# Second input projection on 528 tokens: two 264-column products in place of a 512- and a 16-column one, and one reordering on GpSimd

## The chip, the cores and the metric

The kernel runs on one core of one Trainium2 chip. The metric is device time in microseconds (us) for one execution; lower is better. The core's engines run side by side, each taking its own instructions in order and meeting the others only through semaphores: TensorE (PE, with its weight loads as PEld), VectorE (DVE), ScalarE (ACT), GpSimd (POOL) and SyncE, which issues the DMAs (SP).

## What is computed

A sequence of 512 tokens of width 1024 passes through two layers of a first network and then one layer of a second. The change is in the input projection of the second network's layer. That layer sees 16 further meta tokens ahead of the 512, so keys, values, the forget gate and the pooled branch need 528 columns, while queries are only needed for the 512. Cut to what matters:

```python
n1 = rmsnorm(h, norm1_w)                       # h: 16 meta tokens + 512 tokens
proj = n1 @ w_in                               # 1024 -> q 512 | k 512 | v 512 | fg 8 | u 512
q = rmsnorm(q.reshape(B, L, 8, 64), q_norm_w)  # per head
k = rmsnorm(k.reshape(B, L, 8, 64), k_norm_w)
cum_logf = cumsum(log_sigmoid(fg + b_fgate))
a_out = forgetting_attention(q, k, v, cum_logf)
pooled = trailing_mean(u, window) - u          # windows 2, 4, 8, 16, one per group of 128
p_out = einsum(pooled, w_pool) * pool_scale
h = h + concat(a_out, p_out) @ w_out
```

The reference is float32. The kernel keeps that accuracy by splitting every operand in two: a high part rounded to the fp32r type and a low part that holds the rest. A product is then three fp32r matmuls: high x high, high x low, low x high.

The other place touched is the first network's convolution module: u = a * sigmoid(g), a depthwise convolution of 31 taps, a layer norm.

## The kernel before

Activations lie with features on the partitions and tokens in the free dimension, so a tile is 128 output features by 512 tokens, one PSUM bank (PS has eight banks, 0 to 7). Weights come in blocks of 128 x 1024 floats, that is one output tile of all eight k-steps. A ring of four slots carries them: SP loads `raw`, ACT rounds it to `wh` (the helper `hi(n)`), POOL subtracts to get `wl` (`lo(n)`), PE uses both. Block n may be rounded only once PE is done with block n - 4.

**The stretch changed most.** The second projection, phases `w_in_2` and `w_in_2b`, has on PE: tiles 0 to 3 (queries, entered together with the operand's making), tile 4 (forget gate), 5 to 8 (the pooled branch's u), 9 and 10 (keys of heads 0 to 3), then the small `pool` block (four products with `w_pool`), two further key tiles (heads 4 to 7), and the value stage, where tokens are the stationary side and a 16-row product serves the meta tokens. Each of the nine tiles from 4 on (seven in `w_in_2`, two in `w_in_2b`) is made by `tile(..., meta_out=...)`: 24 products of 512 columns into one bank of four taken in turn (`T % 4`), and, inserted into k-steps 4 to 7, 24 products of 16 columns for the meta tokens into bank 5 or 7 (`meta_bank`). So k-steps 4 to 7 hold three wide and six narrow products. Before the first narrow one PE waits until the evacuation of tile T - 2 is over (`bank_free`).

DVE scales the 512 columns by the row norm (`r2`) on the way out of PSUM; the meta columns are normalised already, so they are copied by an instruction of their own. The head norms of q and k need PE twice more, hooked into the tiles: `head_stat(e)` (sums of squares by eight to ten tiny products) and `head_spread(e)` (four transposes that broadcast 1/rms, in `hexp`, back over the partitions). Between them ACT takes the root (`head_root`) and DVE inverts and expands it (`head_factor`: RECIPROCAL, then COPY to `hexp`; for keys two more for the meta tokens). After the spread DVE multiplies (`head_norm`), ACT rounds (`head_round`) and DVE makes the low part (`head_low`). DVE also does `log_forget`, `prefix_sums`, `pool_tile(i)` (i + 1 additions over 528 columns and a final operation, giving `pooled`), and `pool_out(i)`. ACT's `pool_operand(t)` and a POOL subtraction split `pooled` for PE. All these are written out by hand in one fixed order for each engine; no scheduler moves them.

**The other stretch.** In the convolution module (`pw1`), PE goes through the tiles a0, g0, a1, g1, a2, c0, g2, a3, c1, g3, a4, ... (weights of a and g, and the taps that PE takes, c). DVE forms `tmp`, ACT the sigmoid, DVE `U`, ACT its high part `UH` and next the roundings `hi`, POOL its low part `UL` (`low_u`), then POOL adds up the taps that ACT prepared (`add_taps`) and those of DVE (`add_vector_taps`), with `lo` of coming weight blocks placed between by `lo_to(n)`, which lowers all blocks below n that are not lowered yet. DVE itself works off 18 taps of each tile.

## Time and profile before

| | us |
|---|---|
| median of 3 runs | 1800.65 (1798.9 to 1801.8) |
| the profiled execution's own time | 1802.55 |
| its span in the trace | 1800.8 |
| PE busy | 1769.1 (98%) |
| POOL / DVE / ACT busy | 887.2 / 789.7 / 663.7 |

The page gives busy time by engine over the whole span; the stretches of interest are short (nine tiles of some 1800 us), so they are read from the timeline. A start time in the timeline is exact to 10 ns; the durations of PE's matmuls overlap each other, so the cost of one is the distance from its start to the next start. "idle before" names who released the engine. Granted clock 1.00 is TensorE at 2.4 GHz, 0.50 is 1.2 GHz.

### The profile page before, as it was taken

To read this page: it belongs to the slowest core of one execution; us is meant where nothing else is said; L and a number is where in the kernel's file an instruction comes from. 1 tells how busy PE (TensorE), PEld (TensorE's weight loads), DVE (VectorE), ACT (ScalarE), POOL (GpSimd) and SP (SyncE) were. 2 spreads that over 40 slices of the span, in tenths; PEclk is the share of its full clock that TensorE was granted. 3 is DMA by queue.
4 is the path that set the end of the run, shared out by engine and by line. 5 is a ranking of instruction groups with operands and counts; after the bars stand their busy time and mean duration, and the time that the engine had idled before them with its cause. 6 is when DMAs were issued, how large, how long until landed. Compare 5 with 4: busy or idle time off the path is not lost.

```text
span 1800.8 us, 23006 instructions
## 1 busy us (share of the span) xinstructions
PE 1769.1 (98%) x8243; PEld 1464.7 (81%) x8243; DVE 789.7 (44%) x1230; ACT 663.7 (37%) x1039; POOL 887.2 (49%) x476
## 2 busy tenths in 40 slices
PE   8999999999999989999999999999999999999999
PEld 6887887888888878787888888888779888888887
DVE  6458554201322489755420232247548154444200
ACT  6338543322221456445322222154248432222221
POOL 5457545444444479755444444453235644444442
PEclk9999999999999999999999999999899999999999
DMA  4531123333333122232333233321210233323331
GB/s 172 138 101 58 37 69 105 97 102 94 93 101 98 59 70 97 81 95 70 104 97 102 94 94 103 96 72 35 84 48 1 94 94 94 104 93 93 106 105 70
DMA packets 46073, 158.45 MB, mean 88 GB/s; under 512 B 5744, under 2 KB 6000, under 8 KB 46000
## 3 DMA queue, kind: packets, MB, share of 16 engines
q1 hardware_dynamic: 46000, 157.45, 28.0%
q8 instruction: 49, 0.80, 0.2%
q14 instruction: 24, 0.20, 0.0%
HBM read 153.10 MB, written 2.10 MB: 86 GB/s over the span
## 4 chain that ended last, share of the span: by engine, by line
PE 91%; DVE 4%; ACT 2%; issue 1%; POOL 1%; DMA 0%; SPq 0%; DVEq 0%; POOLq 0%; ACTq 0%
PE PS L1814 27%; PE PS L1816 27%; PE PS L1815 27%; DVE PS L1196 1%; PE PS L1909 1%; PE PS L1904 1%; PE PS L1905 1%; PE PS L2065 1%; PE PS L1824 1%; PE PS L1946 0%; PE PS L1947 0%; PE PS L1856 0%; PE PS L2088 0%; DVE PS L1188 0%; PE PS L2234 0%
## 5 line engine op out<-in xcount | busy, mean ns | idle before, releaser
L526 POOL TENSOR_TENSOR wl<-raw,wh 128x1024 fp32r<-128x1024 f32 x220 | 533.1, 2424 | 630.1 <-ACT wh L719 198.3
L1815 PE MATMUL PS<-XL,wh 128*128 128x512 f32 x1288 | 503.9, 391 | 0.0
L1814 PE MATMUL PS<-XH,wh 128*128 128x512 f32 x960 | 382.2, 398 | 9.4 <-POOL wl L595 5.3
L1816 PE MATMUL PS<-XH,wl 128*128 128x512 f32 x960 | 376.6, 392 | 0.0
L1815 PEld LDWEIGHTS PS<-XL,wh 128*128 128x128 f32 x1288 | 243.4, 189 | 48.3
L1814 PE MATMUL PS<-HH,wh 128*128 128x512 f32 x688 | 267.6, 389 | 0.0
L1815 PE MATMUL PS<-HL,wh 128*128 128x512 f32 x688 | 267.6, 389 | 0.0
L1816 PE MATMUL PS<-HH,wl 128*128 128x512 f32 x688 | 267.6, 389 | 0.0
L1814 PEld LDWEIGHTS PS<-XH,wh 128*128 128x128 f32 x960 | 181.8, 189 | 47.4 <-POOL wl L595 6.2
L705 ACT ACTIVATE wh<-raw 128x1024 fp32r<-128x1024 f32 x123 | 128.6, 1056 | 244.4 <-PE PS L1816 199.4
L1816 PEld LDWEIGHTS PS<-XH,wl 128*128 128x128 f32 x960 | 181.7, 189 | 38.7
L1188 DVE TENSOR_TENSOR tmp<-PS,r 128x512 f32<-128x512 f32 x116 | 80.0, 692 | 252.3 <-PE PS L1816 239.5
L517 POOL TENSOR_TENSOR wl<-raw,wh 128x1024 fp32r<-128x1024 f32 x45 | 109.0, 2430 | 142.1 <-ACT wh L705 142.1
L719 ACT ACTIVATE wh<-raw 128x1024 fp32r<-128x1024 f32 x68 | 72.1, 1061 | 284.3 <-PE PS L1816 284.3
L1814 PEld LDWEIGHTS PS<-HH,wh 128*128 128x128 f32 x688 | 129.1, 188 | 26.9
L1815 PEld LDWEIGHTS PS<-HL,wh 128*128 128x128 f32 x688 | 129.1, 188 | 26.9
L1816 PEld LDWEIGHTS PS<-HH,wl 128*128 128x128 f32 x688 | 129.1, 188 | 26.7
L1814 PE MATMUL PS<-XF,wh 128*128 128x512 f32 x328 | 127.9, 390 | 0.1
L1816 PE MATMUL PS<-XF,wl 128*128 128x512 f32 x328 | 127.6, 389 | 0.0
L974 ACT ACTIVATE wh<-raw 128x1024 fp32r<-128x1024 f32 x56 | 59.4, 1061 | 166.3 <-PE PS L1816 166.3
L1167 ACT ACTIVATE wh<-raw 128x1024 fp32r<-128x1024 f32 x40 | 42.5, 1062 | 159.0 <-PE PS L1816 159.0
L556 POOL TENSOR_TENSOR prob<-prob,cols 128x512 f32<-128x512 f32 (+2 forms) x64 | 57.0, 894 | 40.8 <-DVE cols L1407 40.1
(351 smaller groups left out, 2517.0 us busy)
## 6 DMA issues: line engine op xcount, KB each, us to landing
raw<-weights SPq DMA_DIRECT2D x287, 512.0 KB, 3.5
X<-x_t SPq DMA_DIRECT2D x8, 256.0 KB, 6.7
out_t<-X SPq DMA_DIRECT2D x8, 256.0 KB, 4.6
KH<-rope_h SPq DMA_DIRECT2D x4, 128.0 KB, 4.7
KL<-rope_l SPq DMA_DIRECT2D x4, 128.0 KB, 5.3
QH<-XH SPq DMA_DIRECT2D x16, 32.0 KB, 2.0
QL<-XL SPq DMA_DIRECT2D x16, 32.0 KB, 2.0
pos_i<-positions SPq DMA_DIRECT2D x1, 256.0 KB, 8.9
```

What stands on the lines that cost most here:

```text
L517: pool.tensor_tensor(wl[:, n % RING], raw[:, n % RING], wh[:, n % RING].bitcast(F32), ALU.subtract).then_inc(w_lo, 1)
L526: pool.tensor_tensor(wl[:, j], raw[:, j], wh[:, j].bitcast(F32), ALU.subtract).then_inc(w_lo, 1)
L556: pool.tensor_tensor(p, p, cols[:, u % 4, 2:3].broadcast_to(p.shape), ALU.mult).then_inc(p_done, 1)
L705: sc.activation(wh[:, j], raw[:, j], ACT.Copy).then_inc(w_hi, 1)
L719: sc.activation(wh[:, j], raw[:, j], ACT.Copy).then_inc(w_hi, 1)
L974: sc.activation(wh[:, slot], raw[:, slot], ACT.Copy).then_inc(w_hi, 1)
L1167: sc.activation(wh[:, slot], raw[:, slot], ACT.Copy).then_inc(w_hi, 1)
L1188: return v.tensor_tensor(out, a, b, op)
L1196: return v.scalar_tensor_tensor(out=out, in0=a, scalar=s, in1=b, op0=op0, op1=op1)
L1814: pe.matmul(out, wa, xa, start=start, stop=False)
L1815: pe.matmul(out, wa, xb, start=False, stop=False)
L1816: return pe.matmul(out, wb, xa, start=False, stop=stop)
```

## The change

Nine tiles now treat the 528 tokens as one row. The high and low operand buffers `XH`, `XL` and the meta operands `meta_h`, `meta_l` become views of `XHR`, `XLR`, whose rows are 576 floats long (2304 bytes); the 16 meta columns stand directly before the 512, and the tokens of every row start at a multiple of 256 bytes. Likewise `r2m` holds 16 ones ahead of `r2`.

`wide_tile` makes for each k-step six products of 264 columns: each of the three operand pairs once for columns 0 to 263 and once for 264 to 527, into two adjacent banks. Three pairs of banks, (5,6), (2,3), (0,1), are taken in turn. Before its first product a wide tile waits for the evacuation of the tile that last used its pair (three tiles earlier, mostly). The head norms move to bank 7, the values' meta product to bank 6. DVE takes all 528 columns out with one instruction (`wide_in`), so the nine small ones for the meta columns go.

The hand-written orders change too: `head_spread(4)` stands at k-step 7 in place of 6, those of 5 and 6 at 7 in place of 6 with their `head_stat` at 2 in place of 3; DVE does `head_in(4)` inside `pool_tile(3)`, right after that tile's evacuation, and `head_factor(5)` ahead of `pool_out(2)`; ACT does `head_square(4)` ahead of `pool_operand(3)`; the value stage takes its first four tiles in the order 2, 3, 0, 1.

Some small buffers move into space that is free at the time (`meta`, `meta_n`, `dw_high`, `dw_low`, `meta_x`), and one `memset` of 128 x 16 is added at the start. In `pw1`, POOL lowers the blocks up to a3 (below `n + 7`) before the first tap sums of j = 0, where it was below `n + 5`.

```diff
+        XHR = sb("XHR", [P, KT, ROW], F32R)
+        XLR = sb("XLR", [P, KT, ROW], F32R)
+        XHM, XLM = XHR[:, :, ROW - L2:ROW], XLR[:, :, ROW - L2:ROW]
+        XH, meta_h = XHM[:, :, META:L2], XHM[:, :, 0:META]
...
-                lo_to(n + 5)
+                lo_to(n + 5 if j else n + 7)
...
             pool_operand(2)
             hi(n0 + 12)
+            head_square(4)
             pool_operand(3)
-            head_square(4)
             hi(n0 + 13)
...
+            def wide_in(dst, w, T, done, rows=P):
                 v.wait_ge(blocks_done, done)
-                sig(tt(dst, PS[0:rows, T % 4], r2[0:rows, :], ALU.mult), bank_free, T + 1)
+                sig(tt(in_halves(dst), wide(w, rows), in_halves(r2m[0:rows]), ALU.mult), bank_free, T + 1)
...
-            pool_tile(3)
-            head_in(4, "w_in_2", 9)
+            pool_tile(3, lambda: head_in(4, "w_in_2", 9))
             head_factor(4)
...
-                    if meta_out is not None and k >= KT // 2:
-                        if k == KT // 2:
-                            pe.wait_ge(bank_free, meta_out - 1)
-                        for i in (2 * k - KT, 2 * k - KT + 1):
-                            ins = products(PS[:, meta_bank(T), 0:META], *weight(n, i), meta_h[:, i], meta_l[:, i],
-                                           i == 0, i == KT - 1)
...
+            def wide_tile(n, w, free, hooks={}):
+                open_block(n)
+                pe.wait_ge(bank_free, free)
+                out = wide(w)
+                for k in range(KT):
+                    if k in hooks:
+                        hooks[k]()
+                    w_high, w_low = weight(n, k)
+                    for x, y, first, last in ((w_high, XHM, True, False), (w_high, XLM, False, False),
+                                              (w_low, XHM, False, True)):
+                        for b in range(2):
+                            ins = pe.matmul(out[:, b], x, y[:, k, b * WIDE:(b + 1) * WIDE], start=first and k == 0,
+                                            stop=last and k == KT - 1)
+                ins.then_inc(blocks_done, 1)
...
-                     10: {3: head(4)[0], 6: head(4)[1]}}
+                     10: {3: head(4)[0], 7: head(4)[1]}}
+            emptied = {4: T0, 5: T0 + 3, 6: T0 + 4, 7: T0 + 5, 8: T0 + 6, 9: T0 + 7, 10: T0 + 8}
             for i in range(4, 11):
-                tile(n0 + i, T0 + i, norms.get(i, {}), meta_out=T0 + i)
+                wide_tile(n0 + i, i - 4, emptied[i], norms.get(i, {}))
```

On PE, in tile 4 around its middle, before (L1814 to L1816 are the three products; 16-column ones stand between the 512-column ones):

```order
4037 L1815 MATMUL PS<-XL,wh 128x512
4038 L1816 MATMUL PS<-XH,wl 128x512
4039 L1814 MATMUL PS<-meta_h,wh 128x16
4040 L1815 MATMUL PS<-meta_l,wh 128x16
4041 L1816 MATMUL PS<-meta_h,wl 128x16
4042 L1814 MATMUL PS<-meta_h,wh 128x16
4043 L1815 MATMUL PS<-meta_l,wh 128x16
4044 L1816 MATMUL PS<-meta_h,wl 128x16
4045 L1814 MATMUL PS<-XH,wh 128x512
```

and now, with L1899 the wide products (the row of L2260 is `head_stat(0)`):

```order
4032 L2260 MATMUL PS<-headones,head_q 128x2 x4
4033 L1899 MATMUL PS<-XHR,wh 128x264 x2
4034 L1899 MATMUL PS<-XLR,wh 128x264 x2
4035 L1899 MATMUL PS<-XHR,wl 128x264 x2
4036 L1899 MATMUL PS<-XHR,wh 128x264 x2
4037 L1899 MATMUL PS<-XLR,wh 128x264 x2
4038 L1899 MATMUL PS<-XHR,wl 128x264 x2
```

Every k-step is now the same six products; the narrow ones are gone.

On ACT, between the end of tile 8 and `head_root(4)`, before (`pool_h<-pooled` is `pool_operand`, `wh<-raw` is `hi`, `hcol<-PS` is `head_root`):

```order
505 L705 ACTIVATE wh<-raw 128x1024
506 L1071 ACTIVATE pool_h<-pooled 128x512
507 L1055 ACTIVATE head_q<-head_t 128x528
508 L705 ACTIVATE wh<-raw 128x1024
509 L1062 ACTIVATE hcol<-PS 128x8
```

and now:

```order
505 L727 ACTIVATE wh<-raw 128x1024
506 L1077 ACTIVATE head_q<-head_t 128x528
507 L1093 ACTIVATE pool_h<-pooled 128x512
508 L727 ACTIVATE wh<-raw 128x1024
509 L1084 ACTIVATE hcol<-PS 128x8
```

The square of head 4 went ahead of `pool_operand(3)`; its root stays behind both that and `hi`.

On POOL at the start of `pw1`, before (`wl<-raw,wh` is `lo`):

```order
71 L624 TENSOR_TENSOR UL<-U,UH 128x542
72 L607 TENSOR_TENSOR acc_p<-acc_p,tapped 128x512 x2
73 L595 TENSOR_TENSOR wl<-raw,wh 128x1024
74 L607 TENSOR_TENSOR acc_p<-acc_p,tapped 128x512 x2
75 L635 TENSOR_TENSOR acc_p<-acc_p,taps_sum 128x512 x2
76 L624 TENSOR_TENSOR UL<-U,UH 128x542
77 L595 TENSOR_TENSOR wl<-raw,wh 128x1024
78 L607 TENSOR_TENSOR acc_p<-acc_p,tapped 128x512 x4
79 L635 TENSOR_TENSOR acc_p<-acc_p,taps_sum 128x512 x2
80 L595 TENSOR_TENSOR wl<-raw,wh 128x1024
```

and now:

```order
72 L646 TENSOR_TENSOR UL<-U,UH 128x542
73 L617 TENSOR_TENSOR wl<-raw,wh 128x1024 x2
74 L629 TENSOR_TENSOR acc_p<-acc_p,tapped 128x512 x4
75 L657 TENSOR_TENSOR acc_p<-acc_p,taps_sum 128x512 x2
76 L646 TENSOR_TENSOR UL<-U,UH 128x542
77 L629 TENSOR_TENSOR acc_p<-acc_p,tapped 128x512 x4
78 L657 TENSOR_TENSOR acc_p<-acc_p,taps_sum 128x512 x2
79 L617 TENSOR_TENSOR wl<-raw,wh 128x1024
```

The low parts of g2 and a3 (rows 73 and 77 before) now both follow the first `UL`; that of g3, the last row, stands where it stood.

## Rows read from the trace of the kernel before

**Rows 1.** The page, chain that ended last, shares of the span by engine

```profile
PE 91%; DVE 4%; ACT 2%; issue 1%; POOL 1%; DMA 0%; SPq 0%; DVEq 0%; POOLq 0%; ACTq 0%
```

**Rows 2.** Timeline of PE, tile 4: start, duration (us), engine, line, operation, operands, shapes

```profile
1214.14 0.48 PE L1814 MATMUL PS<-XH,wh 128*128 128x512 f32 x1
...
1214.68 0.39 PE L1816 MATMUL PS<-XH,wl 128*128 128x512 f32 x1
1214.91 0.17 PE L1814 MATMUL PS<-meta_h,wh 128*128 128x16 f32 x1
...
1215.50 0.47 PE L1814 MATMUL PS<-XH,wh 128*128 128x512 f32 x1
```

**Rows 3.** Timeline of PE, products of 256 and 272 columns in the two attentions

```profile
161.41 0.28 PE L2088 MATMUL PS<-PH,VV 128*128 128x256 f32 x1
...
162.25 0.28 PE L2089 MATMUL PS<-PL,VV 128*128 128x256 f32 x1
...
1351.61 0.29 PE L1815 MATMUL PS<-K2L,Q2H 128*128 128x272 f32 x1
...
1351.87 0.22 PE L2054 MATMUL PS<-mask_r,ident_r 128*128 128x128 f32 x1
```

**Rows 4.** Timeline of DVE in the second projection

```profile
1240.45 0.71 DVE L1188 TENSOR_TENSOR pool_a<-u 128x527 f32<-128x527 f32 x1
...
1267.62 1.50 DVE L1636 COPY hexp<-hcol 128x512 f32<-128x512 f32 x1
...
1284.92 0.43 DVE L1636 COPY hexp<-hcol 128x512 f32<-128x512 f32 x1
```

**Rows 5.** Timeline of ACT, from pool_operand(3) to head_root(4)

```profile
1262.74 0.63 ACT L1071 ACTIVATE pool_h<-pooled 128x512 fp32r<-128x512 f32 x1 [6.02 <-DVE pooled L1196]
...
1265.34 1.04 ACT L705 ACTIVATE wh<-raw 128x1024 fp32r<-128x1024 f32 x1
1267.07 0.18 ACT L1062 ACTIVATE hcol<-PS 128x8 f32<-128x8 f32 x1 [0.69 <-PE PS L2234]
```

**Rows 6.** Timeline of POOL, the same stretch

```profile
1263.45 1.29 POOL L669 TENSOR_TENSOR pool_l<-pooled,pool_h 128x512 fp32r<-128x512 f32 x1 [4.24 <-ACT pool_h L1071]
1266.46 2.38 POOL L517 TENSOR_TENSOR wl<-raw,wh 128x1024 fp32r<-128x1024 f32 x1 [1.71 <-ACT wh L705]
```

**Rows 7.** Chain that ended last, in order of time: head_stat(4) on PE

```profile
1266.05 0.98 PE PS L2234 x8
```

**Rows 8.** Timeline of PE, its idle times in the second projection

```profile
1209.11 0.47 PE L1814 MATMUL PS<-XH,wh 128*128 128x512 f32 x1 [0.81 <-DVE head_t L1188]
...
1283.92 0.28 PE L1814 MATMUL PS<-meta_h,wh 128*128 128x16 f32 x1 [2.57 <-DVE sqb L1192]
...
1308.35 0.50 PE L1814 MATMUL PS<-wh,XH 128*128 128x512 f32 x1 [0.99 <-DVE head_t L1188]
```

**Rows 9.** Stretches: length, busy by engine (instructions), PE's granted clock, DMA share, GB/s

```profile
1284.90:1301.80 16.90, 16.90 (x57) 14.10 (x56) 6.09 (x17) 3.07 (x6) 2.36 (x1) 0.50 0.29 96
1308.70:1312.00 3.30, 3.30 (x9) 2.55 (x8) 2.10 (x5) 1.22 (x2) 2.00 (x1) 0.51 0.00 0
```

**Rows 10.** Timeline of PE in pw1: start of a3 and of g3

```profile
656.38 0.50 PE L1814 MATMUL PS<-XH,wh 128*128 128x512 f32 x1 [3.55 <-POOL wl L595]
...
671.07 0.50 PE L1814 MATMUL PS<-XH,wh 128*128 128x512 f32 x1 [1.76 <-POOL wl L595]
```

**Rows 11.** Timeline of ACT and, below it, of POOL in pw1

```profile
637.58 2.00 ACT L705 ACTIVATE wh<-raw 128x1024 fp32r<-128x1024 f32 x2
...
653.97 2.36 POOL L595 TENSOR_TENSOR wl<-raw,wh 128x1024 fp32r<-128x1024 f32 x1
```

**Rows 12.** Chain that ended last in pw1, in order of time, up to g3

```profile
666.11 0.76 DVE U L1196
...
667.46 1.05 ACT wh L705
668.65 2.38 POOL wl L595
```

More of the change, by code:

```diff
@@ L193, in build @@
         lat = at("lat", A, 0, [P, 5, S])
+        meta_n = at("meta_n", A, 29 * KB, [P, KT, META])
+        meta = at("meta", A, 30 * KB, [P, KT, META])
         gate_c = at("gate_c", A, 10 * KB, [P, 4, S])
@@ L226, in build @@
         ln_sq = at("ln_sq", A, 58 * KB, [P, KT, S])
+        dw_high = at("dw_high", A, 84 * KB, [P, KT, PE_TAPS], F32R)
+        dw_low = at("dw_low", nc.lookup_mloc(hexp).addr, KB, [P, KT, PE_TAPS])
         tap_low = at("tap_low", A, 76 * KB, [P, 3, SLOTS, P], F32R)
@@ L414, in head_parts, with bank_pair, wide, in_halves @@
             return H[:, h], L[:, h], headones[:, odd * HD:odd * HD + 1]
-        def meta_bank(T):
-            return (RB, META_BANK)[T % 2]
+        WIDE = L2 // 2
+        PAIRS = ((RB, HB), (2, 3), (0, 1))
+        PAIR_OF = (0, 1, 2, 0, 1, 2, 0, 1, 0)
+        HEAD_NORM, V_META = META_BANK, HB
+        assert TILE0["w_in_2"] % 4 == 1
+        def bank_pair(w):
+            return PS[:, PAIRS[w][0]:PAIRS[w][1] + 1]
+        def wide(w, rows=P):
+            return bank_pair(PAIR_OF[w])[0:rows, :, 0:WIDE]
+        def in_halves(ap):
+            return ap.rearrange("p (b n) -> p b n", b=2)
+        def pool_bank(i):
+            return bank_pair(1 + i // 2)[:, i % 2]
         def result_bank(layer, h):
@@ L502, in _ @@
             pool.memset(hexp[:, 0], 0.0).then_inc(consts, 1)
-            pool.wait_ge(consts, 4)
+            pool.memset(r2m[:, 0:META], 1.0).then_inc(consts, 1)
+            pool.wait_ge(consts, 5)
             pool.affine_select(out=ident[:], in_=ident[:], compare_op=ALU.not_equal, fill=1.0, base=0,
@@ L510, in _ @@
                 rows = slice(half * HD, (half + 1) * HD)
-                pool.wait_ge(consts, 6 + half)
+                pool.wait_ge(consts, 7 + half)
                 pool.memset(headones[rows, rows], 1.0).then_inc(consts, 1)
@@ L1078, in head_round @@
                     H, _, own = head_parts(e, odd)
-                    sc.activation(H[:, tokens], PS[:, HB], ACT.Copy, scale=own).then_inc(head_hi, 1)
+                    sc.activation(H[:, tokens], PS[:, HEAD_NORM], ACT.Copy, scale=own).then_inc(head_hi, 1)
             head_square(0)
@@ L1622, in head_in @@
                 t = head_t[:, e % 4]
-                if e < 4:
-                    out = t[:, 0:S]
-                else:
-                    v.wait_ge(blocks_done, done)
-                    step(v.tensor_copy(t[:, 0:META], PS[:, meta_bank(T), 0:META]))
-                    out = t[:, META:L2]
+                if e >= 4:
+                    wide_in(t, e + 1, T, done)
+                    return
                 v.wait_ge(blocks_done, done)
-                sig(tt(out, PS[:, T % 4], r2[:], ALU.mult), bank_free, T + 1)
+                sig(tt(t[:, 0:S], PS[:, T % 4], r2[:], ALU.mult), bank_free, T + 1)
             def head_factor(e):
@@ L1687, in prefix_sums, with pool_tile @@
                 sig(tt(decay[:, 3], logf[:, 0], f(decay[:, 2]), ALU.subtract), cum_done, 1)
-            def pool_tile(i):
+            def pool_tile(i, between=None):
                 T, done = T0 + 5 + i, n0 + 6 + i
-                v.wait_ge(blocks_done, done)
-                step(v.tensor_copy(u2[:, 0:META], PS[:, meta_bank(T), 0:META]))
-                scaled(u2[:, META:L2], T, done)
+                wide_in(u2[:], 1 + i, T, done)
+                if between:
+                    between()
                 src, w = u2, 1
@@ L1857, in spread, with tile @@
                 ins.then_inc(rb_done, 1)
-            def tile(n, T, hooks={}, meta_out=None, high=XH, bank=None, order=range(KT), begun=False, ring=4):
+            def tile(n, T, hooks={}, high=XH, bank=None, order=range(KT), begun=False, ring=4):
                 if not begun:
@@ L2259, in _ @@
             for i in range(4):
-                open_tile(T1 + i)
+                pe.wait_ge(bank_free, T0 + 9 + i // 2)
                 pe.wait_ge(pool_hi, i + 1)
                 pe.wait_ge(pool_lo, i + 1)
-                ins = products(PS[:, (T1 + i) % 4], *weight(n1, i), pool_h[:, i], pool_l[:, i], True, True)
+                ins = products(pool_bank(i), *weight(n1, i), pool_h[:, i], pool_l[:, i], True, True)
                 ins.then_inc(blocks_done if i == 3 else pool_mixed, 1)
@@ L2278, in _ @@
                         head_stat(7)
-                    for t in range(4):
+                    for t in (2, 3, 0, 1):
                         q = slice(t * P, (t + 1) * P)
                         products(PS[:, (T0 + 2 + t) % 4], XH[:, k, q], XL[:, k, q], *w, k == 0, k == KT - 1)
-                    ins = products(PS[0:META, META_BANK], meta_h[:, k], meta_l[:, k], *w, k == 0, False)
+                    if i == kk == 0:
+                        pe.wait_ge(bank_free, T0 + 2)
+                    ins = products(PS[0:META, V_META], meta_h[:, k], meta_l[:, k], *w, k == 0, False)
                 ins.then_inc(blocks_done, 1)
```

46 lines of the change are left out of this document (19 added, 27 removed).

## The prediction, made before the changed kernel ran

> **What bounds the kernel now.** I read the page's chain first: 91% of what ended last is PE [rows 1], so a microsecond taken from PE's stream counts unless another engine is just behind. The second look was PE's timeline in the nine tiles, from start to start, because PE's durations overlap. In a k-step that carries meta columns, the three 512-column products take 0.77 us, the last two starts 0.23 apart, and the six 16-column ones take from 1214.91 to 1215.50, 0.59 us [rows 2]. So a product 32 times narrower still costs half of a wide one, and the first wide one behind them costs 0.09 more. Such a step is 1.36 us, one without meta columns 3 x 0.228 = 0.68. Third, the places where PE stands still: 0.8 us ahead of tile 4, 2.57 inside the first tile of `w_in_2b`, 1.0 ahead of the value stage at 1308.35 [rows 8]. Fourth, the stretches: after the 2.57 us PE runs 16.9 us at clock 0.50 and has 3.3 us more at 0.51 at the start of the value stage [rows 9].
>
> **Part 1, the products.** Before, a tile is 4 x 1.36 + 4 x 0.68 = 8.18 us plus hooks. After, it is 48 products of 264 columns. The trace has none, but it has both neighbours: 256 columns start 0.84 / 7 = 0.120 us apart, 272 columns 0.26 / 2 = 0.130 [rows 3]. All of these load 128 x 128 weights each time, as the new ones do. I take 0.1225, near the 256-column rows, since that run is of one uniform kind; bounds 0.118 and 0.130. A tile is then 48 x 0.1225 = 5.88. Gain 2.30 a tile, **20.7 us** for nine (bounds 17.5 and 22.6). The rows of 2304 bytes and the halves that start off the 256-byte grid I price at nothing; the 256-column rows are aligned, so the upper bound of 0.130 covers some cost.
>
> A rule that speaks against it: by the Trainium skill, "TensorE: Matmul & The Clock Gate", section LDWEIGHTS, a weight load takes its columns divided by 1.2 GHz, an estimate of 107 ns for 128. Twice as many loads per wide column would set a floor of 48 x 0.107 = 5.1 us a tile. The narrow products show that floor (0.11 us apart), and 5.88 lies above it, so by the page the loads hide and the sum stands.
>
> **Part 2, the stalls that go.** Tile 4 no longer waits for DVE's first evacuation, only for the row norm: 0.8. The 2.57 us [rows 8] were a narrow product waiting in the first tile of `w_in_2b` for `pool_out(3)`, behind `head_low(4)` on DVE, held up by POOL. The new tile waits for `pool_out(1)` at its start, which DVE does right after the pool block's products; that fits. The 1.0 us before the value stage came from waiting for `head_in(7)`; the stage now starts on banks freed by `head_in(6)`. Together **4.4 us**. With these stalls goes the half clock: 16.9 us at half rate did the work of some 9.0, so 7.9, and 3.3 us the work of 1.75, so 1.6: **9.5 us**.
>
> **Part 3, the stalls that come.** DVE, ACT and POOL lose only nine copies of 0.2 us while PE loses a quarter of its time, so their hand-written chains come up against PE. I laid them out from the durations in the rows. Up to tile 9 all hooks are met within 0.2 us each (0.4 in all). The tight one is `head_spread(4)` in tile 10. Count from the end of tile 9:
> - DVE: `head_in(4)` 0.7, then the five additions and final operation of `pool_tile(3)` that are queued behind it, 5 x 0.72 [rows 4]: 4.3.
> - ACT: `pool_operand(3)` 0.65, `hi` 1.04, `head_root(4)` 0.3 with its meta part [rows 5]: at 6.3. The square moved ahead in ACT's order, but the root did not, so it still waits for `pool_operand(3)`.
> - DVE: RECIPROCAL, then the COPY to `hexp`. POOL has meanwhile begun: `pool_l` 1.29 from 5.0, then `lo` 2.38 [rows 6] until 8.7. The COPY takes 1.50 us where POOL runs and 0.43 where it doesn't, and the 1.50 end with POOL's instruction [rows 4, 6]. So it ends at about 9.1, with the two for the meta tokens at 9.6.
> - PE: three k-steps, `head_stat(4)` 1.0 [rows 7], four k-steps: 2.2 + 1.0 + 2.9 = 6.1.
>
> So PE waits **3.5 us** (2 to 4.5). By the Trainium skill, "SBUF — State Buffer", section on the two separate sides, the port pair that VectorE and GpSimd share is locked for a whole instruction; the copy's rows agree. Without that lock the wait would be 2.0 and the sum 1.5 better. One more wait I find is `head_stat(6)`, which needs `head_in(6)`, `head_round(5)` and ACT's square: 0.8. The clock should fall once behind the 3.5 us, as it did behind 2.57 and 3.55 [rows 8 to 10]. The shortest low stretch in the rows is 3.3 us, costing 1.6; it can be longer, as the 16.9 us were, but those began with narrow products, which are gone. I take 1.6 and half of another, **2.4 us** (0 to 8). Sum of the costs: 0.4 + 3.5 + 0.8 + 2.4 = 7.1.
>
> **Part 4, small things.** The value stage does the same products; its meta product waits for `head_in(7)`, which is over by then. Moved buffers and the 16-column memset lie at the start or beside PE: 0 (within 0.3). SP's waits are on `w_lo` and `heads_done`, which only come earlier in the new order, and the four-slot ring still gives a load three tiles' time, 17 us.
>
> **Part 5, POOL in pw1.** PE stood 3.55 us ahead of a3, waiting for `lo`, which POOL began at 653.97 though ACT had rounded both blocks by 639.6 [rows 10, 11]. Now a3 starts at 652.7. But the chain says that this stall was free: what released g3 at 671.07 runs through DVE's `U` (666.11), ACT's `hi`, POOL's `lo` [rows 12], and ahead of that DVE works off its taps without a gap, untouched by PE. The change moves none of it. So PE does a3, waits some 0.9 for c1's rounded weights, does c1, and then stands until the same 671.07, about 6.5 us in place of 1.76. Gain 0. From g3 on PE sets the pace, so a clock that has fallen in those 6.5 us costs in full: some 2.7 us at half rate, **1.3 us lost** (0 to 1.6). Before, the low clock after the 3.55 us lay inside the wait and cost nothing.
>
> **Sum.** 20.7 + 4.4 + 9.5 - 7.1 - 1.3 = 26.2. From the profiled execution's 1802.55 that gives 1776.3. The profiled execution is 1.9 above the median of the runs shown (1800.65), so I say **1774.5**.
>
> **Rivals.**
> - *The clock stays low* (15%). After the 3.5 us the granted clock stays at 0.50 through both key tiles and into the value stage, as it did for 16.9 us before. For: it did so with the same hooks. Against: no narrow products now. It takes back 6 to 8: 1781.
> - *DVE's chain is met* (15%). If DVE gets ahead (its additions fall between POOL's instructions), the 3.5 us shrink and the clock doesn't fall: 4 to 5 better, 1770.
> - *The wide products are slower than their neighbours* (10%): 0.135 to 0.15, by halves that start off the grid. Against: the convolution's products read at every odd offset, and PE's timeline shows their starts hardly further apart. Each 0.01 is 4.3 us, less what the stalls give back: 1781 to 1785.
> - *The other side: the load isn't hidden* (3%). If a second load of the same weights can't slip under a stream of 110 ns, the products are 0.19 apart: a tile is 9.1, 0.9 more than before, 8 for nine, less what goes with the stalls and plus part 5: some 1806. It decides from 8.18 / 48 = 0.170 on. Against: the 272-column rows.
> - *It does nothing* (2%), if DVE paced the stretch: 1800. Against: DVE idles ahead of most of its waits there.
>
> **How the numbers follow.** My forecast has 55%: 1771 to 1779. The range must take in the low clock, the slower products and the met chain: **1769 to 1784**. A measurement of this kernel tells about 0.2%, 3.6 us, from no change. Chances: faster 0.95, within 0.2% 0.02, slower 0.03.
>
> **What would show it.** Right: starts of the 264-column products 0.12 to 0.125 apart; the value stage's first product near 1282 instead of 1308.35; an idle time of 2 to 4.5 us on PE ahead of `head_spread(4)`, released by DVE; g3 still at 671, with 5 to 7 us of idle time ahead of it, and the stretch behind it at clock 0.5. Wrong: g3 earlier than 671 (then part 5 is a gain), products over 0.13 apart, no wait at the spread, or a clock of 1.00 in the phase before and a low one after.

## The result, and the profile after

| | before | after |
|---|---|---|
| median | 1801.2 us (1798.9 to 1801.9, 4 runs) | 1780.1 us (1779.1 to 1780.7, 4 runs) |
| span of the profiled execution | 1800.8 | 1778.9 |

The ratio is 0.9883, 95% interval 0.9864 to 0.9902: the change takes 21 us off. The prediction said 1774.5 (1769 to 1784), faster. The side and the range hold; the middle was 5.6 us too low, and the result lies 1.1 us outside the 1771 to 1779 that I had given my own theory. The sections below say which steps that comes from. Two executions that stood far off the others of their kernel, one of `e3_root_first` (6346.9 us) and one of `e6_four_parts` (2067.4 us, at a mean granted clock of 0.81), are left out of the medians below.

**The products.** PE's timeline in tile 4 of the kernel after (start, duration in us, engine, line, operation, operands, shapes; x2 is both halves of a row):

```profile
1210.22 0.48 PE L1899 MATMUL PS<-XHR,wh 128*128 128x264 f32 x2
1210.55 0.41 PE L1899 MATMUL PS<-XLR,wh 128*128 128x264 f32 x2
...
1211.99 0.40 PE L1899 MATMUL PS<-XLR,wh 128*128 128x264 f32 x2
1212.23 0.40 PE L1899 MATMUL PS<-XHR,wl 128*128 128x264 f32 x2
```

From 1210.55 to 1212.23 seven pairs start in 1.68 us, 0.240 a pair, 0.120 a product. A k-step is 0.72 us, where one that carried meta columns was 1.36 [rows 2] and one without 0.68.

**The waits.** All idle times of PE over 0.4 us between there and the attention (in brackets the idle time and who released it):

```profile
1235.58 1.02 PE L2260 MATMUL PS<-headones,head_q 128*128 128x2 f32 x8 [0.54 <-DVE PS L1218]
...
1261.73 0.23 PE L2269 MATMUL PS<-ident,meta_x 16*128 16x16 f32 x1 [3.85 <-DVE meta_x L1660]
1274.55 0.23 PE L2269 MATMUL PS<-ident,meta_x 16*128 16x16 f32 x1 [0.67 <-DVE meta_x L1660]
...
1278.88 0.20 PE L2258 MATMUL PS<-headones,head_q 128*16 128x2 f32 x2 [1.34 <-ACT head_q L1077]
```

These are `head_stat(3)`, `head_spread(4)`, `head_spread(5)` and `head_stat(6)`. The three of [rows 8] are gone; the value stage's first product starts at 1286.67 with no wait, 21.68 us sooner than at 1308.35. What stands behind the 3.85 us is seen on DVE, ACT and POOL, one after the other:

```profile
1255.95 0.69 DVE L1218 SCALAR_TENSOR_TENSOR pooled<-pool_a,u 128x512 f32<-128x512 f32 x1
1258.46 0.20 DVE L1654 RECIPROCAL hcol<-hcol 128x8 f32<-128x8 f32 x1 [1.82 <-ACT hcol L1088]
1258.70 2.54 DVE L1655 COPY hexp<-hcol 128x512 f32<-128x512 f32 x1
...
1256.68 0.63 ACT L1093 ACTIVATE pool_h<-pooled 128x512 fp32r<-128x512 f32 x1 [3.57 <-DVE pooled L1218]
1257.21 1.04 ACT L727 ACTIVATE wh<-raw 128x1024 fp32r<-128x1024 f32 x1
1258.16 0.16 ACT L1084 ACTIVATE hcol<-PS 128x8 f32<-128x8 f32 x1
...
1258.61 2.35 POOL L539 TENSOR_TENSOR wl<-raw,wh 128x1024 fp32r<-128x1024 f32 x1
```

ACT takes the root only after `pool_operand(3)` and `hi`; the COPY to `hexp` starts 0.09 us behind POOL's subtraction and ends 0.28 us after it, 2.54 us for what took 0.43 in another place [rows 4].

**The clock.** Stretches of the kernel after (length, PE busy, instructions, granted clock, DMA share, GB/s): behind the 3.85 us, behind the 1.34, behind `g3` in pw1, and the whole of the nine tiles.

```profile
1262.80:1266.20 3.40, 3.40 (x11) 0.50 0.32 130
1280.00:1283.30 3.30, 3.30 (x16) 0.50 0.11 19
670.60:675.60 5.00, 4.96 (x12) 0.50 0.72 222
1210.20:1286.60 76.40, 69.98 (x537) 0.96 0.28 91
```

Before, the nine tiles took 99.2 us (1209.11 to 1308.35), with 16.9 of them at half clock [rows 9]; now 76.4, with 6.7 at half clock. The value stage runs at full clock from its first product, and its first product lies 29.4 us ahead of the first score product, against 31.1.

**pw1.** PE there, after the change:

```profile
658.81 0.47 PE L1830 MATMUL PS<-UH,wh 128*128 128x512 f32 x1 [0.92 <-ACT wh L727]
...
670.64 0.79 PE L1830 MATMUL PS<-XHR,wh 128*128 128x512 f32 x1 [5.97 <-POOL wl L617]
671.23 0.63 PE L1831 MATMUL PS<-XLR,wh 128*128 128x512 f32 x1
671.66 0.63 PE L1832 MATMUL PS<-XHR,wl 128*128 128x512 f32 x1
```

`g3` starts at 670.64 where it started at 671.07 [rows 10]. This execution was 0.4 us ahead of the other already at the start of pw1 (DVE's `U` at 665.70, before 666.11 [rows 12]), so `g3` gained nothing. The idle time ahead of it has grown from 1.76 to 5.97 us, and the products behind it are 0.43 us apart, at clock 0.50, for 5 us.

### The profile page after: what moved, and what is told of

It is laid out like the page before. It is cut to its first block, busy times and chain, and to the rows that moved or that the text cites. A ratio compares the mean times of both kernels' runs of the same rounds, so it can differ in the third digit from the quotient of the medians.

```text
span 1778.9 us, 22989 instructions
## 1 busy us (share of the span) xinstructions
PE 1742.8 (98%) x8243; PEld 1448.7 (81%) x8243; DVE 793.2 (45%) x1221; ACT 662.8 (37%) x1039; POOL 886.8 (50%) x477
## 4 chain that ended last, share of the span: by engine, by line
PE 88%; DVE 6%; ACT 3%; issue 2%; POOL 1%; DMA 1%; SPq 0%; DVEq 0%; POOLq 0%; ACTq 0%
PE PS L1830 26%; PE PS L1832 25%; PE PS L1831 25%; PE PS L1899 2%; DVE PS L1218 1%; PE PS L1935 1%; PE PS L1930 1%; PE PS L1931 1%; PE PS L2091 1%; DMA raw<-weights 1%; DVE PS L1210 1%; PE PS L1840 0%; DVE XLR L1218 0%; ACT wh L727 0%; PE PS L2114 0%
## 5 line engine op out<-in xcount | busy, mean ns | idle before, releaser
L1831 PE MATMUL PS<-XLR,wh 128*128 128x512 f32 x1216 | 474.4, 390 | 0.0
L1830 PE MATMUL PS<-XHR,wh 128*128 128x512 f32 x888 | 349.0, 393 | 9.3 <-POOL wl L617 6.0
L1832 PE MATMUL PS<-XHR,wl 128*128 128x512 f32 x888 | 346.8, 391 | 0.0
L1831 PEld LDWEIGHTS PS<-XLR,wh 128*128 128x128 f32 x1216 | 229.2, 188 | 47.3
L1830 PEld LDWEIGHTS PS<-XHR,wh 128*128 128x128 f32 x888 | 167.6, 189 | 45.1 <-POOL wl L617 6.4
L1832 PEld LDWEIGHTS PS<-XHR,wl 128*128 128x128 f32 x888 | 167.4, 189 | 35.1
L1210 DVE TENSOR_TENSOR tmp<-PS,r2m 128x512 f32<-128x512 f32 x116 | 80.0, 691 | 254.7 <-PE PS L1832 241.9
```

What stands on the lines that cost most here:

```text
L1210: return v.tensor_tensor(out, a, b, op)
L1830: pe.matmul(out, wa, xa, start=start, stop=False)
L1831: pe.matmul(out, wa, xb, start=False, stop=False)
L1832: return pe.matmul(out, wb, xa, start=False, stop=stop)
```

## Experiments

For small differences a number needs care here: two traces of one kernel can lie 3 us apart (see the repetition, `c1_changed_again`). I therefore give the medians, and beside them lengths of stretches within a trace: "tiles" is from the first wide product to the first product of the value stage, 76.45 us in the kernel after.

### The reordering in pw1, taken out and done alone

`e1_pw1_undone` is the changed kernel with

```diff
-                lo_to(n + 5 if j else n + 7)
+                lo_to(n + 5)
```

> The changed kernel with its reordering on GpSimd in pw1 undone alone: POOL lowers the blocks below n + 5 before the first tap sums, as in the kernel before. My theory (part 5, now with 2.3 us from the changed kernel's trace): g3 starts near 670.7 either way, since DVE's taps, ACT and POOL lead up to it; with a3 late again (3.5 us of idle, 1.8 ahead of g3) the fall of the clock lies inside the wait, and PE comes out of pw1 some 2 us sooner: about 2 us faster than the changed kernel (1778). Rival: the earlier a3 is worth its 3.5 us, and undoing it makes the kernel slower by 3 to 4 us (1784). Rival: it makes no difference, since what follows in pw1 takes up the 2 us.

Measured 1778.8 us (1778.3 to 1780.4), 1.3 below the changed kernel's 1780.1. Its PE at the same place:

```profile
655.88 0.51 PE L1830 MATMUL PS<-XHR,wh 128*128 128x512 f32 x1 [3.52 <-POOL wl L617]
...
670.56 0.50 PE L1830 MATMUL PS<-XHR,wh 128*128 128x512 f32 x1 [1.74 <-POOL wl L617]
```

and the 5.5 us behind `g3` run at clock 1.00:

```profile
670.50:676.00 5.50, 5.44 (x24) 1.00 0.69 207
```

`g3` starts at the same time whether `a3` waited 3.5 us or not. The second projection starts at 1207.77 in this trace, 1210.22 in that of the kernel after.

`e2_pw1_alone` is the kernel before with the opposite edit.

> The kernel before with the reordering on GpSimd in pw1 alone. My theory: about 2 us slower than the kernel before (1803), g3 at its old start with some 6 us of idle ahead of it and the clock at 0.50 for some 5 us behind it. Rival: faster by 3 to 4 us (1797.5).

Measured 1804.7 us against 1800.0 for the kernel before on the same chip; ratio 1.0034 (1.0016 to 1.0053), so slower. The 4.7 us between the medians is not its price: 4 of its 12 executions took 1811 to 1815 us, where 2 of 23 of the kernel before took 1809 to 1810, and I don't know why. In its trace the idle time ahead of `g3` is 6.00 us, and the start of tile 4 moves from 1209.11 to 1211.07, 1.96 later.

`e9_together_but_pw1` and `e5_again` are a pair on one chip: the improved kernel described below, with and without the change's order in pw1.

> The version with all four edits (1769.6), but with the change's order on GpSimd in pw1. It prices the pw1 reordering beside its counterpart on the same chip. My theory: 2.0 to 2.5 us slower than the version with all four, by the half clock behind g3, 1772. Rival: no difference; the 2.5 us between single traces would then be chance.

Measured 1771.6 (1769.9 to 1773.4) against 1769.0 (1768.6 to 1773.1) for `e5_again`. The intervals of the two ratios overlap widely, so this pair's medians alone would settle nothing. The three differences of medians, 1.3, 4.7 and 2.7 us, have one sign, but not one size. What settles the size is a length inside each trace, from the start of `g3` to the first product of tile 4 (us):

| pair | order of before in pw1 | the change's order | difference |
|---|---|---|---|
| kernel before, `e2_pw1_alone` | 538.04 | 540.39 | 2.35 |
| `e1_pw1_undone`, changed kernel | 537.21 | 539.58 | 2.37 |
| `e5_again`, `e9_together_but_pw1` | 537.28 | 539.65 | 2.37 |

In all six traces `g3` itself starts between 670.0 and 671.1. So the reordering in pw1 costs 2.4 us, the half of the 5 us at clock 0.50. The rival, a gain, has nothing for it.

### The 3.85 us ahead of head_spread(4)

`e3_root_first`, the changed kernel with one step moved on ACT:

```diff
             head_square(4)
+            head_root(4)
             pool_operand(3)
             hi(n0 + 13)
-            head_root(4)
             head_round(4)
```

> The changed kernel with one step moved on ACT: head_root(4) ahead of pool_operand(3). My theory of the 3.85 us that PE stands ahead of head_spread(4): ACT's root waits behind pool_operand(3), which waits for DVE's pool_tile(3); so DVE's COPY to hexp falls into POOL's lo and takes 2.5 us in place of 0.43. With the root first, DVE's RECIPROCAL starts at once after pool_tile(3), its COPY is over before POOL begins, and the spread's wait goes from 3.85 to at most 0.3; the clock no longer falls behind it (1.6 us more). About 4 to 5.5 us faster than the changed kernel (1775). Rival: DVE's additions are the limit, and the wait stays above 2 us. Rival: the wait goes but turns up again at head_spread(5) or head_stat(6) (now 0.67 and 1.34), gain under 2 us.

Measured 1774.6 us (1773.2 to 1775.2; 1775.1 with the execution that is left out). DVE and POOL at the place:

```profile
1259.91 0.43 DVE L1655 COPY hexp<-hcol 128x512 f32<-128x512 f32 x1
1260.37 0.15 DVE L1659 RECIPROCAL hcol<-hcol 16x2 f32<-16x2 f32 x1
1260.56 1.17 DVE L1660 COPY meta_x<-hcol 16x128 f32<-16x128 f32 x1
...
1260.38 1.27 POOL L691 TENSOR_TENSOR pool_l<-pooled,pool_h 128x512 fp32r<-128x512 f32 x1 [4.24 <-ACT pool_h L1093]
```

and PE's two remaining waits, and its clock over the nine tiles:

```profile
1261.79 0.23 PE L2269 MATMUL PS<-ident,meta_x 16*128 16x16 f32 x1 [0.90 <-DVE meta_x L1660]
...
1276.37 0.20 PE L2258 MATMUL PS<-headones,head_q 128*16 128x2 f32 x2 [0.93 <-ACT head_q L1077]
...
1213.20:1282.60 69.40, 67.02 (x537) 1.00 0.32 99
```

The big COPY takes 0.43 us, and the wait falls from 3.85 to 0.90. I had expected at most 0.3: the small copy to `meta_x`, 16 x 128, now falls into POOL's `pool_l` and takes 1.17 us in place of 0.21. The clock doesn't fall at all in this stretch, and the tiles take 69.4 us, 7.0 less: 2.95 from the spread, 0.67 and 0.41 from the two later waits, and 3.3 from 6.7 us that are no longer at half clock, 7.3 in sum. So ACT's order, with the collision that it sets up between DVE and POOL, was the cause, not DVE's additions as such.

`e8_evacuate_late` undoes the change's new order on DVE instead:

```diff
-            pool_tile(3, lambda: head_in(4, "w_in_2", 9))
+            pool_tile(3)
+            head_in(4, "w_in_2", 9)
```

> The changed kernel with one part of its reordering undone on DVE: head_in(4) again behind pool_tile(3), not inside it. It asks what that part is worth. My theory, laid out from the changed kernel's trace: head_t comes 4.2 us later, so PE waits some 4 us already ahead of head_stat(4) in tile 10, and less or nothing at head_spread(4), since root, RECIPROCAL and copies run in PE's four k-steps after it, partly in POOL's lo: 4 to 6 us in all in place of 3.85, time 0 to 3 us above the changed kernel. Rival: it is worth nothing, since DVE's additions end at the same time. Rival: the order before was better: 2 us or more faster.

Measured 1781.5 us (1777.8 to 1784.2). The wait moves to `head_stat(4)`, as laid out:

```profile
1262.65 0.21 PE L2259 MATMUL PS<-headones,head_q 128*16 128x2 f32 x2 [4.33 <-ACT head_q L1077]
```

and there is none left at the spread. The tiles take 76.9 us against 76.45: the waits over 0.4 us sum to 5.8 us in place of 6.4, but the clock is low for some 9.6 us in place of 6.7. As it stands, the early `head_in(4)` of the change shows no gain that one trace could tell. It should be the step that makes the fix above possible, since the root can't be taken before `head_stat(4)`; the root first without the early `head_in(4)` was not run.

### The operand's layout

`e4_rows_528`, the changed kernel with rows of 528 floats, so that the tokens of a row start at 64, 128, 192 or 0 bytes past a multiple of 256:

```diff
-ROW = 4 * META + S
+ROW = L2
```

> The changed kernel with rows of 528 floats in place of 576, so that the tokens of a row no longer start at multiples of 256 bytes, in every phase that reads the operand. My prediction priced the alignment at nothing: products of 264 columns stay 0.120 us apart, those of 512 columns 0.228, time within 2 us of the changed kernel. Rival: products off the grid are slower; already 0.002 us on each of the several thousand products that read this operand would cost some 10 us.

Measured 1800.7 us, ratio to the kernel before 0.9995 (0.9982 to 1.0008): the whole gain is gone. My expectation failed, the rival's held in kind: this layout is slower. Groups of PE's instructions in the stretch 900:1180 (line, operands, shapes, count, busy us, mean ns), first of the kernel after, then of this one:

```profile
L1831 PE MATMUL PS<-HL,wh 128*128 128x512 f32 x255 | 99.2, 389 | 0.0
...
L1831 PE MATMUL PS<-XLR,wh 128*128 128x512 f32 x157 | 61.1, 389 | 0.0
```

```profile
L1831 PE MATMUL PS<-HL,wh 128*128 128x512 f32 x235 | 91.4, 389 | 0.0
...
L1831 PE MATMUL PS<-XLR,wh 128*128 128x512 f32 x174 | 68.8, 396 | 0.0
```

Products that read `HL`, whose layout is the same in both, are unchanged; those that read the operand last longer. By their starts they go from 0.2267 us apart (27 in 6.12 us from 889.68 on) to 0.2315 (26 in 6.02 from 889.82 on). The profile counts 888 k-steps of three such products, 328 in which one of three reads the operand (there too all starts are 0.232 apart), and some 500 more: about 4,150 products by 0.005 us, an estimate of 21 us. They are spread over the whole kernel and no single wait shows them. The 264-column products go from 0.120 to 0.123 (nine pairs in 2.21 us from 1228.06 on), though nearly all of them start off the grid of 256 bytes in both layouts.

What the run shows is the price of the layout, not yet the rule behind it. In k-steps 3 and 7 the rows of this layout start at multiples of 256 bytes, as all rows of the changed kernel do, and these k-steps are no faster: from 889.13 to 923.18 the trace has 49 k-steps in a row, and every one takes 0.69 or 0.70 us, none 0.68. Either products off the grid slow their neighbours too, as the k-steps with one such product in three suggest, or it isn't the start of a row that decides. No run here separates the two.

### What sets the distance of the products

`e7_load_apart` turns the two inner loops round, so that no two products in a row have the same weights:

```diff
-                    for x, y, first, last in (...):
-                        for b in range(2):
+                    for b in range(2):
+                        for x, y, first, last in (...):
```

> The changed kernel with the loops inside a k-step turned round: first the three operand pairs on columns 0 to 263, then the three on 264 to 527, so that no two products in a row have the same weights. My theory: each product loads its weights anyway and the load hides, so the starts stay 0.120 us apart and the time within 2 us of 1780. Rival: two products in a row on the same weights are what makes 0.120 possible, and they go apart to 0.13 or more, 4 us or more slower.

Measured 1780.2 us. The starts are 0.123 us apart (seven from 1212.81 to 1213.67), not 0.120, and the tiles take 77.0 us. That is 0.5 us of 76; the pairing is worth 0.003 us a product and isn't what makes the products fast.

`e6_four_parts` cuts each product in two of 132 columns:

```diff
                         for b in range(2):
-                            ins = pe.matmul(out[:, b], x, y[:, k, b * WIDE:(b + 1) * WIDE], ...)
+                            for c in (0, WIDE // 2):
+                                ins = pe.matmul(out[:, b, c:c + WIDE // 2], x,
+                                                y[:, k, b * WIDE + c:b * WIDE + c + WIDE // 2], ...)
```

> The changed kernel with each 264-column product of the nine tiles cut in two of 132 columns: 96 products a tile. It asks for the floor that a weight load sets. My theory: half as many columns don't halve the distance, since the 16-column products, which load as many weights, start about 0.113 apart; so 0.11 to 0.12 apart here too, a tile of 10.6 to 11.5 us in place of 5.8, and 43 to 51 us more for nine, 1823 to 1831. Rival: the distance follows the columns (0.06), the time stays near 1780, and then the narrow products before were slow for another reason than the load.

Measured 1895.6 us (1895.4 to 1905.4), ratio 1.055 (1.051 to 1.059), far above my 1823 to 1831. The distance is as I said; the clock isn't. PE's timeline early in tile 4 and a little later, four products a row:

```profile
1213.40 0.61 PE L1900 MATMUL PS<-XHR,wh 128*128 128x132 f32 x4
1213.85 0.61 PE L1900 MATMUL PS<-XLR,wh 128*128 128x132 f32 x4
...
1218.79 1.06 PE L1900 MATMUL PS<-XHR,wh 128*128 128x132 f32 x4
1219.65 1.06 PE L1900 MATMUL PS<-XLR,wh 128*128 128x132 f32 x4
```

At first a product takes 0.45 / 4 = 0.112 us, like the 16-column ones before, though it has eight times their columns. By the Trainium skill, "TensorE: Matmul & The Clock Gate", section LDWEIGHTS, loading 128 columns takes an estimated 107 ns; the 0.112 agree. That it is the load and not a fixed price of any product, the two kinds of product of `head_stat` show, both with two columns (kernel after):

```profile
1253.70 0.20 PE L2258 MATMUL PS<-headones,head_q 128*16 128x2 f32 x2
1253.84 1.05 PE L2260 MATMUL PS<-headones,head_q 128*128 128x2 f32 x8
1254.75 0.49 PE L1899 MATMUL PS<-XHR,wh 128*128 128x264 f32 x2
```

With 16 columns of weights to load two products take 0.14 us, 0.07 each; with 128 columns eight take 0.91, 0.114 each. Some 5.5 us after the first product of tile 4 (1212.04), with no idle time ahead of it, the clock falls, and each product then takes 0.213 (12 in 2.56 us from 1218.79 on); at this clock the 107 ns of the Trainium skill don't hold. It stays there:

```profile
1216.00:1220.00 4.00, 4.00 (x29) 0.72 0.71 198
1221.00:1366.00 145.00, 145.00 (x677) 0.50 0.08 23
1366.00:1376.00 10.00, 10.00 (x76) 0.90 0.29 96
```

PE is busy for all of the 145 us of the second line. The clock comes back behind the first 512-column products (the `pool` block from 1363.31 on) and falls again 17 us into the next narrow ones, with PE busy throughout. So here the clock fell twice inside an unbroken stream of narrow products with a weight load each, with no stall ahead of it.

`e10_few_narrow` asks the same of the kernel before, by leaving out 21 of the 24 narrow products of each tile:

```diff
-                        for i in (2 * k - KT, 2 * k - KT + 1):
-                            ins = products(PS[:, meta_bank(T), 0:META], *weight(n, i), meta_h[:, i], meta_l[:, i],
-                                           i == 0, i == KT - 1)
+                        if k == KT // 2:
+                            products(PS[:, meta_bank(T), 0:META], *weight(n, 0), meta_h[:, 0], meta_l[:, 0],
+                                     True, True)
```

> The kernel before with 21 of the 24 products of 16 columns left out in each of the nine tiles (the first k-step's three stay, so keys, values and the rest of the meta tokens come out wrong); waits, hooks and 512-column products are as before. It asks whether the narrow products kept the clock low for 16.9 us behind the stall of 2.57 us. Work taken out: 21 x 0.113 a tile and some 0.09 for each of three returns to 512 columns less, 2.5 to 2.6 a tile, 23 us for nine; the stall of 2.57 us grows by what POOL and DVE don't give back, 2 to 5 us. My theory: with hardly a narrow product left, the clock at 0.50 behind the stall lasts 3 to 5 us in place of 16.9, some 6 us more gained: 1773 to 1777. Rival: the low stretch lasts as long, and its cause is something else (the short pieces of the hooks, the weights just loaded): 1779 to 1783.

Measured 1785.1 us (1783.4 to 1786.6), later than either theory. PE's waits and the stretches behind them:

```profile
1257.65 0.20 PE L2232 MATMUL PS<-headones,head_q 128*16 128x2 f32 x2 [4.42 <-ACT head_q L1055]
...
1275.16 0.28 PE L1814 MATMUL PS<-meta_h,wh 128*128 128x16 f32 x1 [2.71 <-DVE sqb L1192]
```

```profile
1275.10:1278.60 3.50, 3.44 (x12) 0.56 0.50 162
1278.60:1289.10 10.50, 9.41 (x48) 0.98 0.29 100
```

Behind the same stall, 2.71 us here and 2.57 before, ahead of the same instruction, the half clock now lasts 3.4 us in place of 16.9. That was my theory. The 16.9 are no chance of one execution: in the trace of `e2_pw1_alone`, which has all narrow products, the clock is at 0.50 for 16.8 us behind the same stall. The 3.4 rest on one trace. What I had not seen is the new wait of 4.42 us at `head_stat(4)`: the old orders of DVE and ACT can't feed a PE whose tiles are that much shorter, and the wait brings a fall of the clock of its own. The nine tiles take 79.8 us, against 76.45 in the kernel after, though the products of one tile take about as long (an estimate of 24 x 0.2267 + 3 x 0.113 + 0.09 = 5.9 us against 48 x 0.120 = 5.8). So the shorter tiles and the new orders belong together.

### The repetition

> The changed kernel itself once more, so that the small differences of the other runs are taken against it on the same chip: 1780.1, as before. It also asks whether the fall of the clock near 1368 in the attention (some 1.5 us), which the first trace of the changed kernel had, comes again: if it belongs to the kernel's timing, it should; if it comes and goes from run to run, the 1.5 us are no cost of the change.

Measured 1783.3 us (1779.5 to 1783.9, six runs), 3 above the first four, so not 1780.1 again. The stretch in question, of this run and then of the first trace of the kernel after:

```profile
149.80:155.80 6.00, 5.82 (x17) 0.50 0.34 62
```

```profile
147.50:155.80 8.30, 7.85 (x41) 1.00 0.30 68
```

In the first attention the clock falls for 6 us in one execution and not in another of the same program, at the same stall of 1.33 us; it costs 3 us, which is the whole difference between these two traces (tile 4 starts at 1213.28, before at 1210.22). The stall is in all 14 traces, and the clock fell behind it in this one and in that of `e3_root_first`, in no other. The fall near 1370, in the last attention (1.5 us), came again here and in `e1_pw1_undone` and `e10_few_narrow`, but in no other trace. It stands behind a stall of 1.16 us ahead of the product of `PMH` and `VMV`, which waits for `P2L`, and this stall is in all 14 traces. In that of the kernel before it is this row, and no fall follows:

```profile
1391.71 0.39 PE L2093 MATMUL PS<-PMH,VMV 128*128 128x256 f32 x1 [1.16 <-DVE P2L L1188]
```

So the fall comes and goes from one trace to the next at an unchanged stall. Both traces of the changed kernel have it; whether it belongs to that kernel stays open.

### All edits together

`e5_all_together` is the changed kernel with the order of before in pw1, `head_root(4)` first, and:

```diff
-            def pool_tile(i, between=None):
+            def pool_tile(i, between=None, ahead=None):
...
                 assert w == WINDOWS[i]
+                if ahead:
+                    ahead()
                 sig(stt(pooled[:, i], ...), pooled_done, i + 1)
...
-            pool_tile(3, lambda: head_in(4, "w_in_2", 9))
-            head_factor(4)
+            pool_tile(3, lambda: head_in(4, "w_in_2", 9), lambda: head_factor(4))
...
-                     ... 7: {4: head(3)[0]}, ...
+                     ... 7: {5: head(3)[0]}, ...
-                wide_tile(n0 + i, 7 + i, (T1 + 2, T1)[i], {2: head(5 + i)[0], 7: head(5 + i)[1]})
+                wide_tile(n0 + i, 7 + i, (T1 + 2, T1)[i], {2 + i: head(5 + i)[0], 7: head(5 + i)[1]})
```

> The changed kernel with four edits: the reordering in pw1 undone, head_root(4) ahead of pool_operand(3), head_factor(4) ahead of the last operation of pool_tile(3) on DVE, and head_stat(3) and head_stat(6) one k-step later. My theory, in which PE sets the pace: against the root-first kernel (1775.1), 2.0 to 2.5 for pw1 and up to 0.9 + 0.5 + 0.7 for the waits that were left: about 1771. The wait at head_spread(4) goes (0.9 in the root-first kernel, since the small copy to meta_x still fell into POOL's instruction). Rival: the gains don't add, since a stall in pw1 or at the spread is paid again by the clock or by a later wait: 1774 to 1776.

Measured 1769.6 us, ratio to before 0.9828 (0.9806 to 0.9850); the changed kernel on the same chip has 0.9895 (0.9875 to 0.9915). Repeated:

> The version with all four edits once more, as the counterpart of the one before it: 1769.6 again, about 10 us below the changed kernel. It also asks whether the wait of 1.2 us that its first trace showed in the last attention, ahead of a product that reads P2L, belongs to it.

Measured 1769.0, ratio 0.9821 (0.9797 to 0.9845). In the repetition the nine tiles take 67.8 us at full clock, with one wait left over 0.4 us, ahead of `head_spread(3)`; the one that the question was about is in the last attention:

```profile
1238.90 0.66 PE L2272 MATMUL PS<-ident,hexp 128*128 128x128 f32 x4 [0.53 <-DVE hexp L1655]
...
1357.75 0.39 PE L2120 MATMUL PS<-PMH,VMV 128*128 128x256 f32 x1 [1.15 <-DVE P2L L1210]
```

It doesn't belong to this version: the kernel before has the same wait, 1.16 us (above), and so has every other trace. Moving `head_stat(3)` only moved its wait, 0.54 to 0.53, to the spread behind it. It is the fastest version of this study, some 11 us below the changed kernel's first runs and 31 below the kernel before.

## Why the prediction was right, and where it was off

- **Part 1, the products: right, a little low.** 0.120 us apart, predicted 0.1225 (0.118 to 0.130). Nine tiles of 48 give 73.6 - 51.8 = 21.8 us, predicted 20.7. The floor set by the load hides under 264 columns, as said; `e6_four_parts` shows it coming out below that. The layout "priced at nothing" was right for the change as made, but not because the layout is free. It held only with rows of 576 floats, in which every 512-column product starts on the grid; `e4_rows_528` loses the whole gain. The argument that starts at odd offsets cost hardly anything, drawn from the convolution, was misread: in the kernel before, the convolution's products (`UH`, `UL`) start 0.233 us apart (23 in 5.36 us from 641.62 on), where those that read `XH` and `XL` start 0.227 apart. The eye doesn't find that in a timeline, and 0.005 us a product is 20 us over the kernel.
- **Part 2, the stalls that go: right.** The 0.8, the 2.57 and the 1.0 us are gone, and the 16.9 us of half clock. That narrow products had stretched these was half a guess (in part 3); `e10_few_narrow` bears it out, 3.4 us in place of 16.9, in one trace.
- **Part 3, the stalls that come: right in place and cause, too small in size.** `head_spread(4)` 3.85 us against 3.5, by ACT's order and the COPY caught in POOL's `lo`, as laid out, and `e3_root_first` shows it. The others were 0.54 + 0.67 + 1.34 = 2.55 against 1.2: `head_spread(5)` I had found met within the 0.2 of a hook, and `head_stat(6)` took 1.34, not 0.8. In all 6.4 against 4.7. The half clock was 6.7 us long, costing 3.35, against 2.4: not one fall and half a chance of another, but two, the second behind 1.34 us of idle time, less than any that I had taken for one that brings a fall. So the value stage's first product came at 1286.67 and not near 1282.
- **Part 4, small things: not separated.** The bound was 0.3. After all terms, 0.7 us of the projection stay unexplained (21.8 + 13.9 - 6.4 - 3.35 = 25.95; measured from DVE's first evacuation, 1208.27 and now 1210.16, to the first score product, 1339.41 and now 1316.03: 25.3).
- **Part 5, pw1: right in sign and mechanism.** `a3` early gains nothing, `g3` comes at its old time with 5.97 us of idle ahead (predicted 5 to 7), the clock behind it is at 0.50. The cost is 2.4 us, the same in three pairs of traces, predicted 1.3 (0 to 1.6): the half clock lasted 5.0 us, not 2.7, and 1.6 was no upper end.
- **Not in the sum at all**: the fall of the clock near 1370, 1.5 us. It stands behind a stall of 1.16 us that the kernel before has too, without the fall. It was there in both traces of the changed kernel; whether its timing brings it or chance does stays open.
- **The step from one execution to the median.** I took off the 1.9 us by which the profiled execution before stood above its median; after, it stood 0.6 above. 1.3 us of the miss are this.

Sum of the miss: 1.7 + 0.95 + 1.1 + 1.5 + 0.7 + 1.3, less 1.1 for the products and the 0.4 of the head start, is 5.75, against 5.6. All terms but the products and the head start err to the same side: the stalls and the clock behind them were priced too low.

Of the rivals, "the clock stays low" is out (two falls of 3.3 to 3.4 us, each ended by itself; that its 1781 lay nearer to the result than my forecast is luck, since it came there by another way). "DVE's chain is met" didn't happen of itself, but `e3_root_first` makes it happen: the medians differ by 5.5 us, close to what that rival said (4 to 5), the stretch itself by 7.0. "Wide products slower" and "the load isn't hidden" fall with the 0.120; "does nothing" with the result.

## What to carry to other kernels

Where PE sets the pace, count its small products, not their columns: with 128 x 128 weights of its own, a product of 16 or 132 columns took 0.112 us and one of 264 took 0.120, and in one run a long row of the small ones brought the clock to half. Fold leftovers into the wide products, and measure the row length of the operand that streams through PE: here rows of 576 floats, all at multiples of 256 bytes, were free, and rows of 528 cost 20 us. Then expect the hand-written orders of the other engines to be the next limit, and look there for a step that waits behind one it doesn't need: here one step moved on ACT gave another 7 us in its stretch, a third of what the whole change had brought. A block lowered earlier on an engine that isn't the last to arrive buys nothing, and the longer idle time that it makes on PE can cost: 2.4 us here.

## What the runs showed of the hardware

- **Rows of 528 floats in place of 576**, six of eight of which start off a multiple of 256 bytes, put 512-column fp32r products 0.2315 us apart in place of 0.2267 (2%). All three of a k-step go apart when one of them reads such rows, and so do the k-steps whose rows start on the grid. With 264 columns the difference between the two layouts is 0.003 us.
- **Narrow products at both clocks.** With a 128 x 128 load each, 132 columns start 0.112 us apart at clock 1.00 and 0.213 at 0.50; 16 columns in the kernel before 0.113 and 0.213 (1286.10 to 1286.74): the distance goes with the clock and not with the columns. With 16 columns of weights, two-column products take 0.07 us in place of 0.114.
- **The clock fell without a pause**: in `e6_four_parts` behind 5.5 us of such products, and stayed at 0.50 for 145 us of unbroken work, until 512-column products came; the second time it fell 17 us into them. With wide products it came back after 3.3 to 5 us in the stretches shown here, after 6 in the attention.
- **A fall is not fixed by the stall ahead of it.** Behind the same 1.33 us in the first attention it fell in 2 traces of 14, for 6 us, which costs 3; behind the same 1.16 us in the last attention in 4 of 14, which costs 1.5. A difference of 3 us between two kernels should be looked for there before it is explained.
- **DVE's copies beside POOL.** COPY 128 x 512: 0.43 us at its shortest, 2.54 behind a POOL subtraction just begun. COPY 16 x 128: 0.21 and 1.17. By the Trainium skill, "SBUF — State Buffer", section on the two separate sides, one of the two holds the shared ports for its whole instruction; both copies end with POOL's instruction, 0.28 and 0.08 us after it, and the small copy is held like the large one.
